# Split weights written back over the raw ones: a ring of six slots whose loads wait for TensorE, and loops written out

## What is computed

```python
h = rmsnorm(x, g_pre[i]); uz = h @ w_in[i]; u, z = uz[..., :D_INNER], uz[..., D_INNER:]
y = pool_mixer(u, ...) if i % 2 == 0 else rglru(causal_depthwise_conv(u, ...), ...)
o = (y * silu(z)) @ w_out[i]; x = x + rmsnorm(o, g_post[i])
gate = sigmoid(rmsnorm(x, g_ple_in[i]) @ w_ple_gate[i])
x = x + rmsnorm((p[i] @ w_ple[i]) * gate, g_ple_out[i])
...
proj = rms_norm(x, norm_g) @ w_in          # then MLA, SGU and GLA branches
merged = sum(sigmoid(gate_b) * (y_b @ w_branch[b]) for b in range(3))
x = x + merged @ w_out
```

## Time and profile before

| | |
|---|---|
| median of 3 runs | 3858.26 us (3857.76 to 3860.76) |
| the profiled execution | 3862.58 us, of it 3860.8 us span |
| PE busy | 3546.0 us, 92% |
| DVE busy | 2383.1 us, 62% |
| ACT busy | 1634.9 us, 42% |
| POOL busy | 898.1 us, 23% |
| bytes read from HBM | 611 MB, 159 GB/s over the span |

### The profile page before, as it was taken

The page is one execution under the profiler, slowest core; times in us unless marked ns, Lnnn a source line. Parts: engine busy times, 40 slices in busy tenths (PEclk is TensorE's granted clock), DMA queues, the critical chain, the costliest instruction groups (busy, mean ns, idle before and its releaser), DMA issues.

```text
span 3860.8 us, 73979 instructions
## 1 busy us (share of the span) xinstructions
PE 3546.0 (92%) x28672; PEld 3505.5 (91%) x28672; DVE 2383.1 (62%) x3042; ACT 1634.9 (42%) x2019; POOL 898.1 (23%) x904
## 2 busy tenths in 40 slices
PE   7999999879999898795789999999986799999999
PEld 7999999879999897795788999999986698999999
DVE  7766644678788547757555655555658465655554
ACT  4334434443588444443333334443443243444443
POOL 4832311234465212201015200000201115200000
PEclk9999999889999998897889999999998799999999
DMA  5555555345455554450225445555441044555554
GB/s 186 178 186 183 185 199 185 132 147 186 168 182 181 198 193 136 136 178 33 77 97 176 164 173 188 186 187 191 160 164 45 32 149 157 170 191 186 186 186 169
DMA packets 167409, 618.49 MB, mean 160 GB/s; under 512 B 18576, under 2 KB 18704, under 8 KB 166544
## 3 DMA queue, kind: packets, MB, share of 16 engines
q1 hardware_dynamic: 164880, 600.13, 45.3%
q10 hardware_dynamic: 2304, 15.14, 1.0%
HBM read 611.01 MB, written 4.19 MB: 159 GB/s over the span
## 4 chain that ended last, share of the span: by engine, by line
PE 86%; DVE 8%; POOL 2%; ACT 2%; issue 1%; DMA 1%; POOLq 0%; DVEq 0%; ACTq 0%; SPq 0%
PE banks L502 26%; PE banks L508 26%; PE banks L503 26%; PE pm L508 1%; PE pm L503 1%; PE pm L502 1%; DVE wide L1080 1%; DVE xs L1070 1%; DVE scr L1154 1%; POOL win L1637 1%; DVE scr L1192 1%; PE pm L613 1%; PE ms_bank L521 1%; PE pm L644 0%; PE pm L645 0%
## 5 line engine op out<-in xcount | busy, mean ns | idle before, releaser
L1046 DVE TENSOR_TENSOR w_lo<-raw,w_hi 128x1024 fp32r<-128x1024 f32 x1144 | 1486.8, 1305 | 987.3 <-ACT w_hi L762 962.2
L762 ACT ACTIVATE w_hi<-raw 128x1024 fp32r<-128x1024 f32 x1144 | 1204.8, 1057 | 1180.4 <-PE banks L508 1147.5
L502 PE MATMUL banks<-xs,w_hi 128*128 128x256 f32 x5728 | 1430.5, 287 | 108.0 <-DVE xs L1070 99.3
L503 PE MATMUL banks<-xs,w_hi 128*128 128x256 f32 x5728 | 1423.7, 285 | 0.0
L502 PEld LDWEIGHTS banks<-xs,w_hi 128*128 128x128 f32 x5728 | 1111.5, 194 | 116.3 <-issue 76.7
L503 PEld LDWEIGHTS banks<-xs,w_hi 128*128 128x128 f32 x5728 | 1113.3, 194 | 0.3
L508 PE MATMUL banks<-xs,w_lo 128*128 128x256 f32 x5728 | 816.4, 285 | 0.0
L508 PEld LDWEIGHTS banks<-xs,w_lo 128*128 128x128 f32 x5728 | 749.7, 194 | 0.0
L502 PE MATMUL banks<-inner,w_hi 128*128 128x256 f32 (+1 forms) x1408 | 339.2, 280 | 21.6 <-ACT w_hi L762 16.9
L503 PE MATMUL banks<-inner,w_hi 128*128 128x256 f32 (+1 forms) x1408 | 338.5, 280 | 0.0
L502 PEld LDWEIGHTS banks<-inner,w_hi 128*128 128x128 f32 x1408 | 268.3, 191 | 22.2 <-ACT w_hi L762 17.2
(11 more groups left out here) (257 smaller groups left out, 4223.2 us busy)
## 6 DMA issues: line engine op xcount, KB each, us to landing
raw<-weights SPq DMA_DIRECT2D x1144, 512.0 KB, 3.3
wide<-x_in ACTq DMA_DIRECT2D x2, 2048.0 KB, 8.4
x_scratch<-wide ACTq DMA_DIRECT2D x1, 2048.0 KB, 8.5
wide<-x_scratch ACTq DMA_DIRECT2D x1, 2048.0 KB, 7.7
out_x<-wide ACTq DMA_DIRECT2D x1, 2048.0 KB, 6.3
scr<-w_s ACTq DMA_DIRECT2D x2, 512.0 KB, 3.7
scr<-b_s ACTq DMA_DIRECT2D x2, 512.0 KB, 5.4
tab<-tables ACTq DMA_DIRECT2D x1, 836.5 KB, 4.4
```

Source lines behind the costliest of these rows:

```text
L502: nc.tensor.matmul(bank, w_hi[:, slot, w], x[:, 0:T], start=(k + t == 0), stop=False)
L503: nc.tensor.matmul(bank, w_hi[:, slot, w], x[:, T:2 * T], start=False, stop=False)
L762: nc.scalar.activation(w_hi[:, slot, :], raw[:, slot, :], ACT.Copy).then_inc(hi_done, 1)
L1046: nc.vector.tensor_tensor(w_lo[:, slot, :], raw[:, slot, :], w_hi[:, slot, :].bitcast(F32), ALU.subtract).then_inc(lo_done, 1)
```

## The change

`w_lo` now occupies the memory of `raw`: DVE writes the low part over the raw weights. The memory so freed makes six slots instead of four, LOOKAHEAD becomes 5, and the three buffers take the same 48 KB per partition as before. Since `w_lo` is what PE reads last, a slot is free for the next load only when PE has finished the unit in it: the load of unit `n` waits for `pe_mark` of unit `n` - 6, where it waited for `lo_done`. ACT's split waits for the load alone, because the load already waited for PE. All loops over turns are written out on all engines, so that every wait and address is a constant. DVE has one more wait in `vb` and `ub`, for its own result four products back. Cut to its core:

```diff
@@ -29,7 +29,7 @@
 NP_ = PLE // P
 UNIT_TILES = 8
 UNIT = UNIT_TILES * P
-SLOTS = 4
+SLOTS = 6
 LOOKAHEAD = SLOTS - 1
 BANKS = 4
 LRU_BANKS = 6
...
@@ -147,9 +138,10 @@
             return ctx.enter_context(nc.semaphore(name))
 
 
-        raw = sb("raw", [P, SLOTS, UNIT])
+        with ExitStack() as overlay:
+            raw = sb("raw", [P, SLOTS, UNIT], F32, overlay)
+        w_lo = sb("w_lo", [P, SLOTS, UNIT], F32R)
         w_hi = sb("w_hi", [P, SLOTS, UNIT], F32R)
-        w_lo = sb("w_lo", [P, SLOTS, UNIT], F32R)
         xs = sb("xs", [P, ND, 2 * T], F32R)
         val = sb("val", [P, 4, T])
         act = sb("act", [P, 4, T])
...
@@ -373,64 +365,33 @@
         block = ctx.enter_context(nc.Block())
 
 
+        def used(s, i, u):
+
+            return i * len(s.marks) + (s.mark0 + s.marks_to((u + 1) * UNIT_TILES))
+
+        def used_before(s, i, u):
+
+            if u:
+                return used(s, i, u - 1)
+            return used(s, i - 1, s.units - 1) if i else s.mark0
+
         @block.sync
         def _(sp):
-            def load(n, slot):
-                if isinstance(n, int) and n >= n_units:
+            def load(n, freed):
+                if n >= n_units:
                     return
-                wait(sp, lo_done, n - SLOTS + 1)
-                sp.dma_start(raw[:, slot, :], weights[n]).then_inc(raw_in[slot], 16)
+                wait(sp, pe_mark, freed)
+                sp.dma_start(raw[:, n % SLOTS, :], weights[n]).then_inc(raw_in[n % SLOTS], 16)
 
             sp.dma_start(chan[:], channels).then_inc(consts_in, 16)
             for n in range(LOOKAHEAD):
-                load(n, n % SLOTS)
+                load(n, 0)
 
             for s in stages:
-                def turn(i):
+                for i in range(s.turns):
                     for u in range(s.units):
-                        load(i * s.units + (s.unit0 + u + LOOKAHEAD),
-                             (s.unit0 + u + LOOKAHEAD) % SLOTS)
-                static = 1 if s is stages[-1] else 0
-                if s.turns - static > 1:
-                    with sp.Fori(0, s.turns - static) as i:
-                        turn(i)
-                    if static:
-                        turn(s.turns - 1)
-                else:
-                    for i in range(s.turns):
-                        turn(i)
-
-
-        def run_stage(eng, s, turn, per=None, chain=None, unroll=False):
-
-            turn(0)
-            if s.unroll or unroll:
-                for i in range(1, s.turns):
-                    turn(i)
-                return
-            last = 1 if s is stages[-1] else 0
-            n = s.turns - 1 - last
-            if n > 0:
-                with eng.Fori(1, n + 1) as i:
-                    if chain is not None:
-                        with chain.loop(i - 1, n, per):
-                            turn(i)
-                    else:
-                        turn(i)
-            if last:
-                turn(s.turns - 1)
-
-        def used(s, i, u):
-
-            return i * len(s.marks) + (s.mark0 + s.marks_to((u + 1) * UNIT_TILES))
-
-        def used_before(s, i, u):
-
-            if u:
-                return used(s, i, u - 1)
-            if isinstance(i, int) and i == 0:
-                return s.mark0
-            return used(s, i - 1, s.units - 1)
+                        load(i * s.units + (s.unit0 + u + LOOKAHEAD), used_before(s, i, u))
+
 
         def product_end(s, i, j):
 
...
@@ -490,7 +448,7 @@
                     while k < p.depth:
                         u, c = divmod(p.first_tile + k, UNIT_TILES)
                         n = min(p.depth - k, UNIT_TILES - c)
-                        slot = (s.unit0 + u) % SLOTS
+                        slot = (i * s.units + s.unit0 + u) % SLOTS
                         unit = i * s.units + (s.unit0 + u + 1)
                         if c == 0:
                             pe.wait_ge(hi_done, unit)
...
@@ -753,12 +712,12 @@
 
         @block.scalar
         def _(sc):
-            def split_hi(n, slot, free):
-
-                if isinstance(n, int) and n >= n_units:
+            def split_hi(n):
+
+                if n >= n_units:
                     return
-                sc.wait_ge(raw_in[slot], (n - slot) * 4 + 16)
-                wait(sc, pe_mark, free)
+                slot = n % SLOTS
+                sc.wait_ge(raw_in[slot], n // SLOTS * 16 + 16)
                 nc.scalar.activation(w_hi[:, slot, :], raw[:, slot, :], ACT.Copy).then_inc(hi_done, 1)
 
             def feed(f, gain, first):
...
@@ -955,7 +914,7 @@
                 def turn(i):
                     for u in range(s.units):
                         n_ = s.unit0 + u + LOOKAHEAD
-                        split_hi(i * s.units + n_, n_ % SLOTS, used_before(s, i, u))
+                        split_hi(i * s.units + n_)
                         if s.name == "lru":
                             h, q = divmod(u, 5)
                             if q == 0:
...
@@ -1038,10 +998,11 @@
         def _(ve):
             link = lambda ins: dve_chain.link(ve, ins)
 
-            def split_lo(n, slot):
-
-                if isinstance(n, int) and n >= n_units:
+            def split_lo(n):
+
+                if n >= n_units:
                     return
+                slot = n % SLOTS
                 ve.wait_ge(hi_done, n + 1)
                 nc.vector.tensor_tensor(w_lo[:, slot, :], raw[:, slot, :], w_hi[:, slot, :].bitcast(F32),
                                         ALU.subtract).then_inc(lo_done, 1)
...
@@ -1373,6 +1334,8 @@
                         if s.name in ("latent", "vb", "ub"):
                             wait(ve, pool_done if s.name == "latent" else inner_ready,
                                  (s.base["p"] if s.name == "latent" else gelus * 8) + m - 3)
+                        if s.name in ("vb", "ub") and m >= 4:
+                            ve.wait_ge(res_ready, s.base["q"] + m - 3)
                         nc.vector.tensor_tensor(v, product(s, i, j), rstd_x[:], ALU.mult)\
                             .then_inc(dve_read, 1)
                     elif s.name in ("rope_k", "gqk", "gv", "uq", "ukv"):
...
@@ -1717,15 +1680,11 @@
                         def group_turn(i):
                             for j in range(4):
                                 post(i, j, group)
-                        if group == 0:
-                            group_turn(0)
-                            group_turn(1)
-                        else:
-                            with gp.Fori(2 * group, 2 * group + 2) as i:
-                                with pool_chain.loop(i - 2 * group, 2, 4 * (group + 2)):
-                                    group_turn(i)
+                        for i in (2 * group, 2 * group + 1):
+                            group_turn(i)
                 elif s.name not in ("pooled", "plain", "rope_k", "gqk", "gv", "uq", "ukv", "wo"):
-                    run_stage(gp, s, turn, 16 if s.name == "lru" else 4, pool_chain)
+                    for i in range(s.turns):
+                        turn(i)
                 if s.name == "vb":
                     square_v(6)
                     square_v(7)
```

More of the change, by code:

```diff
@@ L15 @@
-from contextlib import ExitStack, contextmanager
+from contextlib import ExitStack
 import numpy as np
@@ L91, in __init__ @@
     def __init__(self, sem):
-        self.sem, self.base, self.step, self.turn, self.per = sem, 0, 0, 0, 0
+        self.sem, self.steps = sem, 0
     def link(self, eng, ins):
         ins.then_inc(self.sem, 1)
-        self.step += 1
-        eng.wait_ge(self.sem, self.base + self.turn * self.per + self.step)
-    @contextmanager
-    def loop(self, turn, count, per):
-        self.base += self.step
-        self.step, self.turn, self.per = 0, turn, per
-        yield
-        assert self.step == per, (self.step, per)
-        self.base += count * per
-        self.step, self.turn, self.per = 0, 0, 0
+        self.steps += 1
+        eng.wait_ge(self.sem, self.steps)
 def wait(eng, sem, value):
-    if not isinstance(value, int) or value > 0:
+    if value > 0:
         eng.wait_ge(sem, value)
@@ L430, in used_before, with _ @@
                 return used(s, i, u - 1)
-            if isinstance(i, int) and i == 0:
-                return s.mark0
-            return used(s, i - 1, s.units - 1)
+            return used(s, i - 1, s.units - 1) if i else s.mark0
+        @block.sync
+        def _(sp):
+            def load(n, freed):
+                if n >= n_units:
+                    return
+                wait(sp, pe_mark, freed)
+                sp.dma_start(raw[:, n % SLOTS, :], weights[n]).then_inc(raw_in[n % SLOTS], 16)
+            sp.dma_start(chan[:], channels).then_inc(consts_in, 16)
+            for n in range(LOOKAHEAD):
+                load(n, 0)
+            for s in stages:
+                for i in range(s.turns):
+                    for u in range(s.units):
+                        load(i * s.units + (s.unit0 + u + LOOKAHEAD), used_before(s, i, u))
```

(12 more changed lines are left out.)

16 lines of the change are left out of this document (3 added, 13 removed).

## The result

| | before | after |
|---|---|---|
| median, same chip | 3859.51 us (3857.76 to 3863.67, 4 runs) | 3920.59 us (3913.01 to 3924.16, 4 runs) |
| ratio, 95% interval | | 1.0154 [1.0136, 1.0172] |
| the profiled execution | 3862.58 us, span 3860.8 | 3921.99 us, span 3920.2 |

What follows compares the result with a forecast made beforehand. PE was taken to bound the kernel, with the ring a follower. Costs of 69 us less gains of 13 gave +56 on the 3858.3 us median, about 3914 us, slower; range 3878 to 3950.

Steps and rivals of the forecast that it cites:

- The load moves into the unit: Every unit: load starts about +0.2 us, ACT's split +3.5, DVE's read about +5.8 instead of +3.07, 2.75 us late.
- The sum: Whole kernel: costs of 69 us less gains of 13 us, net +56 us, slower.
- Ends of stages: Where PE waits for reads after a stage's last unit: late reads cost 38.6 us, including 6.6 after ukv.
- `plain`: Both plain stages: reads behind the split cost 6.4 us in steps plus 2.5 at the root, 8.9 each, 17.8 together.
- `uq` and `ukv`: Units of uq and ukv: PE waits 0.42 us per unit for a bank, 5 us per layer, 10 in all.
- What two more units win: Waits for split weights at squared, pooled and latent shrink: gain 12.5, say 13 us, with 3.4 of clock.
- `pooled`: In pooled, PE's 2.6 us wait for w_lo goes, counted as a gain.
- The loops: Writing out loops on all engines: taken as 0, bounds 0 to some 3 us won at POOL's and ACT's tails.
- Covered ends: Rival: at stage ends POOL or ACT is late anyway, so the gain stands, 3845 us, faster; chance 0.07.
- Half of the delay: Rival: faster landings or POOL's and ACT's queues cover half of the 69 us, giving 3880 us; chance 0.07.
- The clock: Rival: gaps in plain, uq and ukv lower PE's clock, up to 70 us more, half gives about 3950; chance 0.13.

Runs made afterwards that it cites:

- the queue's order: Changed kernel with reads before splits, and each stage's last split held until its tail and the next feed are done (not after silu, lru): 3852.67 us, ratio 0.9983.
- The kernel with the stage ends: Changed kernel with reads ahead of the split only in the last unit of each stage other than plain, uq and ukv: 3918.69 us.
- before's second profile: Profile of the kernel before, run again unchanged as a kernel of its own: 3861.51 us, ratio 1.0003.
- the late load: Changed kernel with each load sent one unit later, when PE ends unit u instead of u - 1: 4095.95 us, ratio 1.0607.

## Why the prediction was right, and where it wasn't

**The load moves into the unit: right.** Split at +3.36 (I had +3.5), DVE's read at +5.59 (+5.8), landing 3.3. That this is the cause is shown from three sides: the wait alone makes the loss (four slots), a unit more for the load removes it, and the queue's order removes it.

**The sum: close in part by luck.** The kernel with the loops alone has before's ring. Against it the changed kernel is 72 us slower (3920.6 less 3848.8), where costs less gains of the ring were put at 56. So the ring costs some 16 us more net than forecast (the intervals allow about 10 to either side), and the loops, put at 0, gave 10 of them back. The terms below say where they lie as far as is known.

**Ends of stages: right, 28 to 35 us against 32.** The wait after `gate` grew by 2.49 us against 2.75. One part of the reasoning was too narrow: I named the last DVE read as what stands behind the split. The kernel with the stage ends showed that all of the chain's instructions on that engine count, the second step too.

**`plain`: mechanism right, size wrong.** The term of 8.9 us per stage measured 7.0 and 3.7. I let each load start with PE's unit; it is sent when PE ends the unit before, and while PE itself waits the load is already on its way. ACT in the first `plain` stage, as the earlier trace rows:

```profile
693.54 1.06 ACT L721 ACTIVATE w_hi<-raw 128x1024 fp32r<-128x1024 f32 x1 [2.92 <-DMA raw<-weights]
694.51 1.19 ACT L937 ACTIVATE gated<-banks 128x256 f32<-128x256 f32 x4
...
699.34 0.38 ACT L937 ACTIVATE gated<-banks 128x256 f32<-128x256 f32 x1 [0.90 <-PE banks L466]
699.74 1.28 ACT L746 ACT_TABLE_LOAD   x1
```

PE's gaps in it, in its timeline, are three:

```profile
682.84 0.39 PE L460 MATMUL banks<-xs,w_hi 128*128 128x256 f32 x1 [0.74 <-ACT wide L937]
685.57 0.39 PE L460 MATMUL banks<-xs,w_hi 128*128 128x256 f32 x1 [1.76 <-ACT gated L937]
694.93 0.39 PE L460 MATMUL banks<-xs,w_hi 128*128 128x256 f32 x1 [1.86 <-ACT gated L937]
```

4.4 us against 3 x 2.13 = 6.4; in the second `plain` stage there are two, 1.38 and 1.24 us. And the last unit's split is done early enough for its last read to wait for PE (0.90), not for the split, so that the 2.5 us at the root are not there. In the windows above PE's idle time (length less busy) grew from 10.8 us to 14.1 and 13.5, so by 3.3 and 2.7; the rest of the 7.0 and 3.7 is the clock. From start to start, the first three units together are 6.5 us longer than before in the first stage and 3.8 in the second; the 6.5 agree with my 6.4 by luck, since the clock is in them. The last unit with the root is 0.5 us longer in the first and 0.1 shorter in the second, where I had 2.5.

**`uq` and `ukv`: 15.6 against 16.6 us by stage lengths,** but a few us to either side in them belong to the attention work in one execution. Without it: the 24 units other than the first of `uq` and the last of `ukv` are 8.1 us longer in sum, 0.34 each, where I had 0.42; and PE's wait after `ukv` grew by 2.7 and 3.0 us, where I had 3.3. With `plain` the three measured 25.6 us where I had 34.4.

**What two more units win: too high.** PE's wait for `w_hi` did fall (17.5 to 9.9 us; I had 12). Yet 6.4 us of the first `squared` stage in before's profile were the slow pace (60 of its 64 units, 0.107 us each), no wait. Where both kernels ran at the quick pace, the first `squared` stage took 180.8 us in before's second profile and 183.4 after, the second 188.1 and 189.7 against 185.0: 0.6 to 2.2 us won in all, where I had 8.9 with the clock. At the first `squared` PE waits 6.3 us for `w_hi` after the change, against 4.4 and 4.8 in before's two profiles; at the second 3.6 against 12.4 and 12.6. So the two more units paid at one of the two places only. Against a ring of four slots whose loads wait for PE as well (the kernel with the load's wait alone) the changed kernel is 13 us faster, but there PE waits 25.6 us for `w_hi` and 5.3 for `w_lo`, against 17.5 and 2.6 in before, so most of that gain undoes a loss that before did not have.

**`pooled`: the sign was wrong.** I counted the 2.6 us for `w_lo` as a gain. DVE, at the change from `window`:

```profile
231.06 0.43 DVE L1398 TENSOR_TENSOR inner<-act,inner 128x256 fp32r<-128x256 f32 x1
231.41 1.22 DVE L1007 TENSOR_TENSOR w_lo<-raw,w_hi 128x1024 fp32r<-128x1024 f32 x1
232.54 0.54 DVE L1330 TENSOR_SCALAR wide<-banks,chan 128x256 f32<-128x256 f32 x1
```

DVE is held by POOL's last tile of `window` until 230.7, its queue then holds a split ahead of the first bank read, and PE waits 4.4 us for this read (L1330, above). That order is the same in before, where the split starts at 226.61 and the read at 227.75; there PE stopped one product earlier, for `w_lo`. With five units in hand the weights were safe; the bank wasn't. And POOL ends that tile 13.0 us after PE has begun `pooled`, where it was 10.7 (10.0 with the loops alone, 13.8 with the load's wait added to them): the end of `window` is one more end of a stage that came late, by 2.3 us, and my list didn't have it. Against before's second profile, where `pooled` took 89.9 us and not 91.5, the stage is 4.6 us longer.

**The loops: 0 was too low,** for before's ring at least: 10 us, interval 3 to 17, with the bound at 3. By the Trainium skill ("Runtime: NRT & Kernel Launch", § Instruction fetch mechanics) a taken branch whose target lies outside the fetched window stalls the engine; this run agrees in sign. That fetching is the cause isn't shown. PE shows no stall at a turn of a loop: in `silu` of before the unit at each turn's end takes 2.88 us, like the others; for the other engines no row settles it. Only 1.6 of the 10 us can be placed: both `plain` stages take 22.1 us in this kernel, and 22.9 in both profiles of before. At their end PE waits for DVE's first write of `xs`. In before, POOL's copy (L1588) starts 0.01 us ahead of this write, and the write takes 1.30 us; with the loops written out the copy starts 0.05 us behind it, and the first write takes 0.48 us and the second 1.26. So the write that begins under the start of POOL's copy is the slow one, and the order of the two decides whether PE waits for it. The six-slot kernel with the splits three ahead has its loops written out too and measures 0.9999. What the loops are worth in a six-slot kernel stays open.

**The rivals.** Covered ends: excluded. Half of the delay: excluded. The clock: some 5 us of it in `plain`, far from the 36 of its case, but 15 there with the gaps of the late load. The total, 61 us against 56, came out with the errors in `plain` (7 us less than forecast), `squared` and `pooled` (14 to 15 more at equal pace) and the loops (10 less) partly cancelling.

## What to carry to other kernels

A buffer that is freed by a later hand (TensorE's last read in the place of VectorE's split) moves the start of its load, and the number of slots says nothing about that: count the time from the release to the first instruction that needs the load, and compare it with the landing. Throughput can be ample on all engines and the kernel still lose at every place where the bound engine waits for something that stands, on an engine that takes its instructions in order, behind the instruction that waits for the load; it is mended by using the prefetched work one unit later than it is loaded, or by putting it behind all of the urgent chain, the tail too. If a rearrangement recovers less than expected, look at what it has put behind the wait in its turn.

## What the runs showed of the hardware

**Two paces of PE at one granted clock.** In `pooled`, `squared`, `uq`, `ukv` and `wo`, where PE's moving operand is not `xs`, a unit of 24 matmuls takes 2.72 us in some executions and 2.83 in others, nearly always for a whole stage, at a granted clock of 1.00 and without waits, and the same kernel, even one execution of it, shows both (windows above). It is worth 64 x 0.107 = 6.8 us in one `squared` stage. With `xs` it is 2.88 us in all 14 profiles. It changes at a wait: in before the first two units of that stage took 2.74 and 2.72 us, and all from the wait for `w_hi` on 2.83. What decides it I don't know. It is about as large as the gains told apart here, and a single profile should not be used for them.

**Half pace after a gap.** With gaps of 4.6 us in each unit of `plain` most of each burst ran at half pace (1503.05 to 1506.6 in matmuls 0.215 us apart at a granted clock of 0.50, against 0.12 at 1.00), at a mean granted clock of 0.65 over the stage; with the changed kernel's gaps of 0.7 to 1.9 us some matmuls ran so too, 3.8 us' worth in the first `plain` stage and 1.0 in the second.
